# POOL in place of Vector for the low part of a normed tile

## What is computed

```python
for i in range(DEPTH):                                   # 2
    mix = hybrid_mixer(x, ...)                            # ends in @ w_out
    x = layer_norm(ALPHA * x + mix, ln1_g[i], ln1_b[i])   # the first norm
    ffn = jnp.square(jax.nn.relu(x @ mlp_w1[i])) @ mlp_w2[i]
    ple = jax.nn.sigmoid(x @ pe_gate[i] + pe_gate_b[i]) * (p[i] @ pe_proj[i])
    x = layer_norm(ALPHA * x + ffn + ple, ln2_g[i], ln2_b[i])

def layer_norm(x, g, b):
    mu = xf.mean(-1, keepdims=True)
    var = jnp.square(xf - mu).mean(-1, keepdims=True)
    return (xf - mu) * lax.rsqrt(var + LN_EPS) * g + b
```

## Time and profile before

| | |
|---|---|
| median of 3 runs | 4060.84 us (4057.0 to 4062.63) |
| the profiled execution | 4065.51 us, its span 4063.7 us |
| TensorE busy | 3667.1 us, 90% of the span |
| Vector, Scalar, POOL busy | 46%, 23%, 24% |
| mean granted TensorE clock | 0.908 |

### The profile page before, as it was taken

One profiled execution on the slowest core, in us unless ns is written; L12 is line 12 of the kernel. 1 busy time (PEld: TensorE's weight loads), 2 busy tenths in 40 slices (PEclk: granted clock), 3 DMA queues, 4 the chain that ended last, 5 costly groups with the idle time before them and its releaser, 6 DMA issues.

```text
span 4063.7 us, 60832 instructions
## 1 busy us (share of the span) xinstructions
PE 3667.1 (90%) x23288; PEld 2636.0 (65%) x23288; DVE 1864.7 (46%) x3137; ACT 950.9 (23%) x1681; POOL 978.4 (24%) x844
## 2 busy tenths in 40 slices
PE   7889888798899999999988898877989999999997
PEld 3444445488657888888734444456867578888884
DVE  4388887443351222222326888864442512222224
ACT  2121211344221222111121112114431212112222
POOL 1042222154211222222100421232632112222221
PEclk9877886699899999999997888857999999999998
DMA  3100000000111111111010000000001111111110
GB/s 112 33 12 11 16 11 11 17 1 1 32 47 37 47 46 47 51 46 50 33 43 24 16 11 16 16 6 13 0 1 45 38 47 47 49 44 52 46 46 42
DMA packets 38005, 128.27 MB, mean 32 GB/s; under 512 B 7264, under 2 KB 7776, under 8 KB 36960
## 3 DMA queue, kind: packets, MB, share of 16 engines
q1 hardware_dynamic: 37568, 125.29, 9.5%
q10 hardware_dynamic: 288, 1.05, 0.1%
HBM read 120.04 MB, written 5.24 MB: 31 GB/s over the span
## 4 chain that ended last, share of the span: by engine, by line
PE 56%; issue 30%; POOLq 6%; DVE 2%; POOL 2%; ACT 1%; DVEq 1%; DMA 1%; ACTq 0%; SPq 0%
PE bank L982 13%; PE bank L983 13%; PE bank L984 13%; PE bank L707 3%; PE wide L575 2%; PE wide L580 1%; PE bank L652 1%; PE wide L707 1%; PE bank L675 1%; PE wide L638 1%; POOLq L1416 1%; PE bank L871 1%; POOLq L1286 1%; POOLq L1327 1%; PE bank L930 1%
## 5 line engine op out<-in xcount | busy, mean ns | idle before, releaser
L1415 POOL TENSOR_TENSOR WL<-WR,WH 128x1024 fp32r<-128x1024 f32 x160 | 388.8, 2430 | 1496.6 <-ACT WH L1229 1495.9
L605 PE MATMUL bank<-X,WR 128*128 128x512 f32 x1152 | 568.3, 651 | 20.9 <-ACT X L1043 9.9
L982 PE MATMUL bank<-XH,WH 128*128 128x512 f32 x1280 | 517.5, 404 | 19.5 <-DVE XL L1461 10.0
L984 PE MATMUL bank<-XH,WL 128*128 128x512 f32 x1280 | 501.6, 392 | 0.0
L983 PE MATMUL bank<-XL,WH 128*128 128x512 f32 x1280 | 501.6, 392 | 0.0
L605 PEld LDWEIGHTS bank<-X,WR 128*128 128x128 f32 x1152 | 236.8, 211 | 327.4 <-issue 296.5
L1801 DVE TENSOR_TENSOR Y<-Y,bank 128x512 f32<-128x512 f32 x256 | 176.0, 687 | 491.9 <-PE bank L984 491.9
L982 PE MATMUL bank<-HH,WH 128*128 128x512 f32 x1024 | 400.3, 391 | 0.0
L983 PE MATMUL bank<-HL,WH 128*128 128x512 f32 x1024 | 398.7, 389 | 0.0
L984 PE MATMUL bank<-HH,WL 128*128 128x512 f32 x1024 | 398.5, 389 | 0.0
L1788 DVE TENSOR_TENSOR RB<-RB 128x512 f32<-128x512 f32 x128 | 88.6, 692 | 561.3 <-ACT RB L1255 561.3
(11 more groups left out here) (265 smaller groups left out, 5342.9 us busy)
## 6 DMA issues: line engine op xcount, KB each, us to landing
WR<-in_w SPq DMA_DIRECT2D x128, 512.0 KB, 3.5
WR<-in_w_in SPq DMA_DIRECT2D x36, 512.0 KB, 3.5
WR<-in_w_out SPq DMA_DIRECT2D x16, 512.0 KB, 3.5
WR<-in_w_gate SPq DMA_DIRECT2D x16, 512.0 KB, 5.9
Y<-in_xT SPq DMA_DIRECT2D x2, 2048.0 KB, 13.5
out_T<-X SPq DMA_DIRECT2D x1, 4096.0 KB, 11.1
UQ<-in_w_uq SPq DMA_DIRECT2D x2, 1024.0 KB, 7.4
PE_IN<-in_pT SPq DMA_DIRECT2D x2, 1024.0 KB, 4.9
```

What stands on the lines that cost most here:

```text
L605: mm = e.matmul(BK_[hf], WR[:, i % RING, kt, :], X[:, kt, hs(hf)], start=kt == 0, stop=kt == KT - 1)
L982: e.matmul(BK_[b], WH[:, s, w, :], high[:, kt, q], start=kt == 0, stop=False)
L984: mm = e.matmul(BK_[b], WL[:, s, w, :], high[:, kt, q], start=False, stop=kt == kts - 1)
L1415: e.tensor_tensor(WL[:, s, :, :], WR[:, i % RING, :, :], WH[:, s, :, :].bitcast(F32), ALU.subtract)
```

## The change

In the first norm of each layer the 16 subtractions that make XL leave Vector's pipeline and stand in POOL's program, behind POOL's squares of the same norm. Each waits for the same count of `high_x` as before and adds one to the same `low_x`. Vector's pipeline has two steps fewer in each half. The `high_before` argument goes.

```diff
@@ gpsimd
                     split_low(i)
                     if i == ZW + N_WOUT + 1:
                         layer_norm(L * 2 + 1)
+                        for n in range(2 * KT):
+                            hf, kt = n // KT, n % KT
+                            e.wait_ge(high_x, L * 2 * KT + (n + 1))
+                            e.tensor_tensor(XL[:, kt, hs(hf)], Y[:, kt, hs(hf)], XH[:, kt, hs(hf)].bitcast(F32),
+                                            ALU.subtract).then_inc(low_x, 1)
@@ vector, layer_norm
-                        for n in range(KT + 3):
+                        for n in range(KT + 1):
                             if n < KT:
                                 e.tensor_tensor(Y[:, n, q], Y[:, n, q], RST[:, hf, :], ALU.mult).then_inc(ln_xn, 1)
                             if 1 <= n <= KT:
                                 gain, offset = affine(n - 1)
                                 e.tensor_scalar(Y[:, n - 1, q], Y[:, n - 1, q], gain, offset, ALU.mult, ALU.add)\
                                  .then_inc(ln_out, 1)
-                            if n >= 3:
-                                kt = n - 3
-                                e.wait_ge(high_x, high_before + (hf * KT + kt + 1))
-                                e.tensor_tensor(XL[:, kt, q], Y[:, kt, q], XH[:, kt, q].bitcast(F32), ALU.subtract)\
-                                 .then_inc(low_x, 1)
                             e.drain()
```

More of the change, by code:

```diff
@@ L1431, in _, with layer_norm @@
         def _(e):
-            def layer_norm(u, between=None, affine=None, high_before=0):
+            def layer_norm(u, between=None, affine=None):
                 for hf in range(2):
@@ L1770, in _ @@
                          .then_inc(d_free[b], 1)
-                layer_norm(L * 2 + 1, affine=lambda kt: (par_col("l1g", kt), par_col("l1b", kt)), high_before=L * 16)
+                layer_norm(L * 2 + 1, affine=lambda kt: (par_col("l1g", kt), par_col("l1b", kt)))
                 for mt in range(KT):
```

## The result

The changed kernel takes 4069.28 us (median of 18 runs, 4064.6 to 4076.13), the kernel before 4060.18 us (18 runs beside them, 4051.69 to 4068.38). The ratio is 1.0023 with a 95% interval of 1.0015 to 1.003, so +6 to +12 us. I had said 4068.0, which is +7.2.

The account below looks back on a forecast made before the run. PE bounds the kernel, and the second half's last XL ends the stretch where it waits. 2.8 us per layer, 5.6 in both, plus 1.6 for the clock gave +7.2 on 4060.84: 4068.0 us, range 4059.5 to 4073.5.

Parts of the forecast that it names:

- the mechanism: Vector saves its XL but loses time waiting for POOL's at the shared ports: +7.2 us in all, chance 0.70.
- a sum below 8 us: The main mechanism's outcome of 4062.5 to 4069 us, no change that can be told: chance 0.48, against 0.22 above.
- XL on POOL takes 1.26 us: Each XL subtraction on POOL lasts 1.26 us, from rows of 1265 ns for two SBUF inputs of 128x512.
- The first half gives nothing: In each layer's first half Vector's savings go in waits; the second reciprocal starts at 1191.69, as before.
- 0.90 us per XL: Each POOL XL among Vector's multiplies and gains holds Vector up 0.90 us; six per half make 5.40.
- 2.60 us for the last two XL: After the second half's last gain POOL makes two XL in a row, 0.08 + 2 x 1.26 = 2.60 us.
- Cover in the first half: The first half's last XL comes 2.5 us later, but PE's delay is hidden before its wait for second-half XL(3).
- Cover of WL: WL of output tile 2, queued on POOL behind the 16 XL, keeps its gap of 2.9 us, costing nothing.
- The clock: A granted clock of 0.50 at the end of the second half's waits costs 0.8 us per layer, +1.6 in all.
- the one with the clock's fall in full: Clock falls fully at the wait's end in both layers: 5.6 + 3.4 = +9.0, 4069.8 us; no separate chance.
- The wait of a whole instruction: Each POOL XL costs Vector its whole 1.26 us: +7.2 per layer, +14.3 in all, 4075.1 us; chance 0.12.
- The no-wait rival: Vector isn't held up beside POOL's XL, and POOL is the bound: -5.5 us per layer, 4049.9 us; chance 0.08.

Follow-up runs that it names:

- e6: The changed kernel with four extra matmuls on PE ahead of each wait for a second-half XL from tile 3 on: 4067.88 us, ratio to before 1.0013.
- e1: The kernel before, XL still on Vector, plus spare subtractions of two SBUF tiles on POOL that nobody waits for: 4093.25 us, ratio 1.008.
- e5: The changed kernel with the reciprocal, by which Vector multiplies, in PSUM instead of SBUF: 4051.84 us, ratio to before 0.9973.
- e8: The kernel before with the first norm's gain and offset moved from Vector to Scalar, XL and multiply staying on Vector: 4056.96 us, ratio 0.998.
- e9: The kernel before, XL on Vector, with only the reciprocal in PSUM: 4060.27 us, ratio 0.9999.
- e10: Against the kernel before: XL on POOL, gain and offset on Scalar, reciprocal in PSUM: 4053.87 us, ratio 0.9982.
- e11: The kernel before with gain and offset on Scalar, reciprocals in PSUM, XL on Vector, second reciprocal ahead of the first half's XL: 4054.66 us, ratio 0.9985.
- e2: The kernel before, XL still on Vector, plus spare zero fills of 128x1024 on POOL that read nothing: 4070.13 us, ratio 1.0024.

## Why the prediction came out right, and where it was off

The forecast was +7.2 us for a measured +9.1, in range, and the mechanism was the one that I gave the largest chance. Within it I had held a sum below 8 us, no change that can be told, for twice as likely as one above, and it came out above. Step by step, per layer:

- **XL on POOL takes 1.26 us.** Right (1.26 to 1.29 undisturbed, up to 1.75 behind a Vector instruction).
- **The first half gives nothing.** Right: the second reciprocal at 21.54 for 21.19, +0.35.
- **0.90 us per XL.** This is the term that was too small. In the first half the stalls are 0.91 (multiply, 1.60 - 0.69) and 0.95 (gain), and 1.07 for the sixth, which makes the +0.35. In the second, where I had assumed the same mix, it is the gain every time, at 1.61 - 0.54 = 1.07. From tile 0's gain to the last gain's end I had 8.07 + 5.40 = 13.47; the trace has 1206.74 - 1192.24 = 14.50. The squares in rows 8, from which I took 0.90, stood in a queue: each had itself waited behind a Vector instruction (1.44 us apart for 1.04), so that, as I read it, its start had passed when it got its turn. In the second half each XL follows Scalar's rounding, comes at the same place in Vector's step and takes its undisturbed 1.29 us, and the gain pays for all of that but 0.22. The sixth XL of the first half fits: it took 1.26, undisturbed, and it is the one that cost 1.07.
- **2.60 us for the last two XL.** Right: 1209.34 - 1206.74 = 2.60. Together the last XL ends 4.2 us later, where I had 2.8.
- **Cover in the first half.** Right: PE enters the second half at 32.9 for 30.1 and then waits for XL as before. **Cover of WL**: right, WL ends at 1212.78 + 2.80 = 1215.58 and PE begins the tile at 1218.47, a gap of 2.9 us.
- **The clock.** I had 0 to 1.7 and took 0.8. It fell at the end of the second half in both layers, and cost 1.1: the last XL's end to the next tile's start takes 1.50 us for 0.85, and that tile 7.64 for 7.20. e6 removed the fall.
- The sum is 4.15 + 1.1 = 5.25 per layer, 10.5, for my 5.6 + 1.6. The two shares missing are 2.7 from the stalls (0.35 and 1.03 per layer) and 0.6 from the clock. So against the stretch the forecast is 3.3 us short, and against the runs, whose interval holds both, 1.9.

Of the rivals, the one with the clock's fall in full has the nearest number, +9.0, but by luck: its last XL moves too little (5.6 us for 8.3) and its clock costs too much (3.4 for 2.2). The wait of a whole instruction (+14.3) was nearer than I thought: I had set 1.0 us per XL as the line from which it decides, and the second half has 1.07 of 1.29, over that line and short of the whole.

The Trainium skill, SBUF — State Buffer, Who interferes with whom, says that where both engines need the shared port pair, the second to issue fully blocks until the first is done. The traces agree that the gain ends only after the XL does, by 0.28 us for its 0.54 alone; that its other 0.26 passed beside the XL is how I read the difference. By the same rule whoever issues first gets the ports, and the starts in this profile don't show that order: the gain starts 0.04 us ahead of the XL and loses.

The no-wait rival is out by the gains of 1.61 us in the changed kernel itself, and by e1, where 0 stands beside +32.

What stays open: e5 and e8 gained more in the runs (-6 to -16 and -4 to -12 us) than the stretch shows in their profiles (-3.6 and -2.9). Stages that no edit touched differ by some 5 us from one execution to the next, so this may be chance, but no run here settles it.

## What to carry to other kernels

Moving work from Vector to POOL pays only where the instructions that then run side by side do not both need the shared SBUF port, so look at Vector's neighbours in time and count a stall of nearly the whole POOL instruction (here 0.91 to 1.07 us of 1.26 to 1.29) for each that has two SBUF inputs or is a gain and offset of this form. An operand in PSUM takes a two-input instruction out of the conflict at no cost that these runs show (e9, ratio 0.9999), and the reciprocal kept its 3.35 us beside all that POOL did. Without the conflict POOL's XL were as good as Vector's, and no better: the last mark is 51.3 us in e10 and in e11. And work that is released by a step of Vector's own pipeline meets that pipeline at the same place every time, so price the worst instruction of the step, not the mean.

## What the runs showed of the hardware that I had not expected

- The start in the profile does not say who gets the port. A gain at 1192.94 lost to an XL at 1192.98 and took 1.61 us; in e1 a subtraction at 1185.16 instead waited behind a multiply that had started at 1185.11 and took 1.77.
- A fill on POOL that reads nothing holds up Vector's gain (1.35 us for 0.54) and not its two-input instructions (0.67 to 0.69, e2).
- Scalar's Identity with a gain and an offset per partition takes 0.81 us and 1.41 for two behind each other, its Copy of the same tile 0.63 (e8, the changed kernel).
- The granted clock fell to 0.50 after waits of PE in which it did one tile in 2.3 us, and not when the same waits were filled with matmuls (e6).
